# Moving the pw1 pair of chunk five, half B, behind the pw2 product of half A, in a two-layer Conformer and differential-attention trunk

## Reference

```python
def conformer_conv(h, pw1_w, pw1_b, dw_w, dw_b, ln_g, ln_b, pw2_w, pw2_b):
    u = h @ pw1_w + pw1_b                       # 1024 -> 2048
    a, gate = jnp.split(u, 2, axis=-1)
    u = a * jax.nn.sigmoid(gate)
    u = lax.conv_general_dilated(u, dw_w[:, None, :], ..., padding=((30, 0),),
                                 feature_group_count=1024) + dw_b      # causal, 31 taps, per channel
    u = jax.nn.silu(layernorm(u, ln_g, ln_b))
    return u @ pw2_w + pw2_b                    # 1024 -> 1024

x = x + conformer_conv(rmsnorm(x, conv_norm_g), ...)
x = x + (silu(h @ w1) * (h @ w3)) @ w2          # h = rmsnorm(x, ffn_norm_g); 2816 hidden channels
```

## Time and profile before

| | |
|---|---|
| median of 3 runs | 2310.55 us (2309.19, 2310.55, 2311.31) |
| profiled execution | span 2310.0 us (the page gives no other time of its own) |
| PE busy | 2252.5 us, 98% |
| DVE busy | 1673.4 us, 72% |
| ACT busy | 903.3 us, 39% |
| chain that ended last | PE 89%, DVE 8%, ACT 1%, issue 1% |
| HBM | 87 GB/s over the span |

### The profile page before, as it was taken

How to read it: one execution, slowest core, us unless ns; L and a number is a source line. 1 busy time by engine, 2 the same in 40 slices (tenths; PEclk the granted TensorE clock), 3 DMA queues, 4 the chain that set the end, 5 groups by cost and what they waited for, 6 DMA issues and landing times.

```text
span 2310.0 us, 27735 instructions
## 1 busy us (share of the span) xinstructions
PE 2252.5 (98%) x10517; PEld 1826.9 (79%) x10517; DVE 1673.4 (72%) x2617; ACT 903.3 (39%) x1597; POOL 68.6 (3%) x51
## 2 busy tenths in 40 slices
PE   7999989999999999999999999999999999999998
PEld 6885768888888888887777777878788888887886
DVE  6997689999666634345677777674778888877874
ACT  5221532222354422223455555564443332325443
POOL 0000000000000000002111111000000000000000
PEclk9999999999999999999999999999999999999999
DMA  4110223333333333333111111111023333329552
GB/s 141 47 37 19 73 72 93 96 93 95 94 98 91 101 95 95 103 89 84 37 37 37 37 37 37 62 60 44 28 81 101 100 107 105 104 98 325 195 163 88
DMA packets 287666, 202.13 MB, mean 88 GB/s; under 512 B 9045, under 2 KB 254126, under 8 KB 287534
## 3 DMA queue, kind: packets, MB, share of 16 engines
q1 hardware_dynamic: 287534, 200.36, 28.4%
HBM read 174.37 MB, written 25.95 MB: 87 GB/s over the span
## 4 chain that ended last, share of the span: by engine, by line
PE 89%; DVE 8%; ACT 1%; issue 1%; DMA 0%; SPq 0%; DVEq 0%; ACTq 0%
PE ps L2271 27%; PE ps L2273 26%; PE ps L2272 26%; PE ps L2409 3%; PE ps L2254 3%; DVE cacc L1620 2%; DVE cvA L1620 2%; PE ps L2367 1%; DVE sc L1871 1%; PE ps L2326 0%; DVE Wl L1545 0%; ACT sc L1297 0%; DVE Sl L1786 0%; PE ps L2336 0%; DVE rstd L1558 0%
## 5 line engine op out<-in xcount | busy, mean ns | idle before, releaser
L2271 PE MATMUL ps<-Sh,Wl 128*128 128x512 f32 x1616 | 655.8, 406 | 16.4 <-DVE Sl L1708 6.8
L2273 PE MATMUL ps<-Sh,Wh 128*128 128x512 f32 x1616 | 632.7, 392 | 0.0
L2272 PE MATMUL ps<-Sl,Wh 128*128 128x512 f32 x1616 | 631.9, 391 | 0.0
L2271 PEld LDWEIGHTS ps<-Sh,Wl 128*128 128x128 f32 x1616 | 305.1, 189 | 94.6 <-issue 33.3
L2273 PEld LDWEIGHTS ps<-Sh,Wh 128*128 128x128 f32 x1616 | 304.6, 188 | 65.8
L2272 PEld LDWEIGHTS ps<-Sl,Wh 128*128 128x128 f32 x1616 | 305.3, 189 | 59.7 <-issue 3.4
L1545 DVE TENSOR_TENSOR Wl<-raw,Wh 128x1024 fp32r<-128x1024 f32 (+1 forms) x178 | 213.3, 1198 | 87.2 <-ACT Wh L1084 86.3
L1084 ACT ACTIVATE Wh<-raw 128x1024 fp32r<-128x1024 f32 (+1 forms) x178 | 183.3, 1032 | 153.3 <-DMA raw<-in_ffn_w_dram 126.2
L2271 PE MATMUL ps<-G0h,Wl 128*128 128x512 f32 x352 | 138.6, 394 | 0.0
L2273 PE MATMUL ps<-G0h,Wh 128*128 128x512 f32 x352 | 137.0, 389 | 0.0
L2272 PE MATMUL ps<-G0l,Wh 128*128 128x512 f32 x352 | 137.0, 389 | 0.0
(11 more groups left out here) (273 smaller groups left out, 3869.6 us busy)
## 6 DMA issues: line engine op xcount, KB each, us to landing
raw<-in_ffn_w_dram SPq DMA_DIRECT2D x130, 512.0 KB, 3.8
raw<-in_pw_w_dram SPq DMA_DIRECT2D x32, 512.0 KB, 3.9
raw<-in_ffn_w_dram SPq DMA_DIRECT2D x32, 448.0 KB, 3.7
draw<-in_ffn_w_dram SPq DMA_DIRECT2D x55, 256.0 KB, 4.5
raw<-in_ffn_w_dram SPq DMA_DIRECT2D x36, 256.0 KB, 4.2
graw<-t_dram SPq DMA_DIRECT2D x36, 256.0 KB, 4.9
graw<-g_dram SPq DMA_DIRECT2D x33, 256.0 KB, 4.3
g_dram<-st SPq DMA_DIRECT2D x27, 256.0 KB, 2.0
```

Source lines behind the costliest of these rows:

```text
L2271: pe.matmul(dst, ll, rh, start=start, stop=False)
L2272: pe.matmul(dst, lh, rl, start=False, stop=False)
L2273: return pe.matmul(dst, lh, rh, start=False, stop=stop)
```

## The change

The pair of products (5,B) is taken out of the first stage. Its two weight blocks are loaded a second time as blocks AGAIN and AGAIN + 1 behind the eight pw2 blocks, and its two products run behind pw2 of half A and ahead of F0A, into banks 6 and 7. The sum over partitions for half A's norm stands inside the first of these products, after four of its eight chunks. The gate's sigmoid is the last thing ACT does ahead of F0A and goes to sq; the glu (`glu_behind`) is done by DVE in step 0 of F0A. `slot` and `slot_before` keep the ring: the two blocks take slots 2 and 3, behind the last two pw2 blocks, so that the first two F0A blocks keep slots 0 and 1. Splits are placed by hand: `lo(AGAIN)` after pw2_out of chunk 6, `lo(AGAIN + 1)` and `lo(F0A.block0)` ahead of the reciprocal, `lo(F0A.block0 + 1)` in the middle of the Sl loop; on ACT `hi(AGAIN + 1)` and `hi(F0A.block0)` stand ahead of the root, around the loading of its table.

```diff
@@ -96,7 +96,8 @@
 
 PW1 = 0
 PW2A = PW1 + 2 * KC
-F0A = Ffn(0, (LA,), (8, 7, 7), PW2A + KC, 5 * KC, 0, 0, 0, True)
+AGAIN = PW2A + KC
+F0A = Ffn(0, (LA,), (8, 7, 7), AGAIN + 2, 5 * KC, 0, 0, 0, True)
 PW2B = F0A.block0 + F0A.blocks()
 F0B = Ffn(0, (LB,), (8, 7, 7), PW2B + KC, F0A.result0 + F0A.results() + KC, FC, 0, 3 * KC, False)
 ATT0 = F0B.block0 + F0B.blocks()
@@ -196,9 +197,19 @@
     return UBANKS[q % len(UBANKS)]
 
 
+def slot(b):
+
+    return (b if b < AGAIN else b + 2) % RING
+
+
+def slot_before(b):
+
+    return b - {AGAIN: 2, AGAIN + 1: 2, AGAIN + 2: 6, AGAIN + 3: 6}.get(b, RING)
+
+
 def uslot(q):
 
-    return (q + 2 * (TAIL % RING)) % USLOTS
+    return (q + 2 * slot(TAIL)) % USLOTS
 
 
 def down_slot(d):
@@ -222,17 +233,29 @@
 DIAGS = 22
 
 
+BEHIND = LATE - 1
+
+
 def pair(n, hf):
 
-    return 2 * n + hf if n < LATE else 2 * LATE + 2 * hf + n - LATE
+    return PAIRS1.index((n, hf))
+
+
+PAIRS1 = [(n, hf) for n in range(BEHIND) for hf in (LA, LB)] + [(n, LA) for n in range(BEHIND, KC)] + \
+    [(n, LB) for n in range(LATE, KC)] + [(BEHIND, LB)]
+
+
+def pair_before(n, hf):
+
+    return pair(n - 2 if (n, hf) == (LATE, LB) else n - 1, hf)
 
 
 def results_through(b):
 
     if b < PW2A:
-        return 2 * pair(b // 2, LB) + b % 2 + 1
+        return 2 * pair(b // 2, LA if b // 2 == BEHIND else LB) + b % 2 + 1
     if b < F0A.block0:
-        return 4 * KC + b - PW2A + 1
+        return 4 * KC - 2 + b - PW2A + 1
     if b < PW2B:
         return F0A.result0 + b - F0A.block0 + 1
     if b < F0B.block0:
@@ -703,10 +726,10 @@
             return HEADS - 1 if WO0 <= b < WO0 + KC else KC
 
         def ring_hi(b):
-            return Wh[b % RING][:, 0:down_size(b), :]
+            return Wh[slot(b)][:, 0:down_size(b), :]
 
         def ring_lo(b):
-            return Wl[b % RING][:, 0:down_size(b), :]
+            return Wl[slot(b)][:, 0:down_size(b), :]
 
         def step_done(engine, d):
 
@@ -938,6 +961,8 @@
 
             for n in range(KC):
                 load(PW2A + n, cols(pw2, n))
+            load(AGAIN, cols(pw1, KC + BEHIND))
+            load(AGAIN + 1, cols(pw1, BEHIND))
             ffn(F0A)
             for n in range(KC):
                 load(PW2B + n, cols(pw2, n))
@@ -1070,14 +1095,14 @@
 
                 if b >= BLOCKS:
                     return
-                s = b % RING
+                s = slot(b)
                 n = down_size(b)
                 if ATT0 <= b < WO0:
                     act.wait_ge(raw_ok, b - ATT0 + 1)
                 else:
                     act.wait_ge(raw_in[b % 2], 16 * (b // 2 + 1))
                 if b >= F1.block0 + RING or RING <= b < F1.block0:
-                    act.wait_ge(mm, results_through(b - RING))
+                    act.wait_ge(mm, results_through(slot_before(b)))
                 elif b >= F1.block0:
 
                     act.wait_ge(wo_mm, result_at(KC - 4 + s, LB) + 1 if s else 4 * KC)
@@ -1120,7 +1145,7 @@
             def gate(n, hf):
                 act.wait_ge(mm, 2 * pair(n, hf) + 1)
                 if n:
-                    act.wait_ge(u_ok, pair(n - 1, hf) + 1)
+                    act.wait_ge(u_ok, pair_before(n, hf) + 1)
                 act.activation(tmp[:, hf, :], ps[:, 2 * hf, :], ACT.Sigmoid,
                                bias=col("pw1_b", KC + n)).then_inc(sig_ok, 1)
 
@@ -1134,6 +1159,8 @@
                     if n == 1 and hf == LA:
                         act.wait_ge(lam_s, 2)
                         act.activation(lexp, lsum, ACT.Exp).then_inc(lam_e, 1)
+                    if (n, hf) == (BEHIND, LB):
+                        continue
                     gate(n, hf)
                     if n in (1, 2):
                         x_copies(8 * (n - 1) + 4 * hf)
@@ -1181,13 +1208,21 @@
             gate(CONV_PE, LB)
 
             for n in range(KC):
-                hi(PW2A + n + 2)
+                if n < KC - 1:
+                    hi(PW2A + n + 2)
                 squares(SUM_F0A, n, X(n, LA), x_ok, n + 1)
+            hi(AGAIN + 1)
             act.activation(spare, eps, ACT.Sqrt)
+            hi(F0A.block0)
             root(1, LA, SUM_F0A)
             for n in range(KC):
                 act.wait_ge(fx_ok, n + 1)
                 act.activation(Sh[:, LA, n, :], tmp[:, n % 4, :], ACT.Copy, scale=col("ffn_norm_g", n)).then_inc(s_hi, 1)
+                if n == 3:
+                    hi(F0A.block0 + 1)
+            act.wait_ge(mm, F0A.result0 - 1)
+            act.wait_ge(acc_ok, squares_added(SUM_F0A, KC - 1))
+            act.activation(sq[:, 0, :], ps[:, 6, :], ACT.Sigmoid, bias=col("pw1_b", KC + BEHIND)).then_inc(sig_ok, 1)
 
             def ffn(f, beside):
                 for i, (g, what, c, b) in enumerate(f.order()):
@@ -1635,7 +1670,7 @@
                         dve.tensor_tensor(neg_lam, lexp[:, 1:2], lexp[:, 0:1], ALU.subtract).then_inc(lam_s, 1)
                         dve.wait_ge(lam_s, 4)
                         dve.tensor_scalar(neg_lam, neg_lam, -LAMBDA_INIT, None, ALU.add).then_inc(lam_s, 1)
-                    if i == 8 and n < LATE:
+                    if i == 8 and n < BEHIND:
                         glu(n, LB)
                     if n + 2 < KC:
                         lo0, lo1, glu0 = (16, 24, 28) if n + 1 < LATE else (9, 16, 14)
@@ -1683,17 +1718,22 @@
             glu(CONV_PE, LB)
 
             def pw2_out(hf, n):
-                r = (F0A.result0 if hf == LA else F0B.result0) - KC + n
+                r = (F0A.result0 - 2 if hf == LA else F0B.result0) - KC + n
                 dve.wait_ge(mm, r + 1)
                 dve.scalar_tensor_tensor(X(n, hf), by_block(ps[:, n % 4, :]), col("pw2_b", n), X(n, hf),
                                          ALU.add, ALU.add).then_inc(x_ok, 1)
 
             for n in range(KC):
-                lo(PW2A + n + 2)
+                if n < KC - 2:
+                    lo(PW2A + n + 2)
                 pw2_out(LA, n)
                 if n >= 2:
                     add_square(SUM_F0A, n - 1)
+                if n == KC - 2:
+                    lo(AGAIN)
             add_square(SUM_F0A, KC - 1)
+            lo(AGAIN + 1)
+            lo(F0A.block0)
             recip(1, LA)
             dve.wait_ge(rstd_ok, 2)
             for n in range(KC + 2):
@@ -1707,6 +1747,15 @@
                     dve.wait_ge(s_hi, OP_F0A * KC + m + 1)
                     dve.scalar_tensor_tensor(Sl[:, LA, m, :], tmp[:, m % 4, :], col("ffn_norm_g", m),
                                              Sh[:, LA, m, :].bitcast(F32), ALU.mult, ALU.subtract).then_inc(s_lo, 1)
+                if n == 5:
+                    lo(F0A.block0 + 1)
+
+            def glu_behind():
+
+                dve.wait_ge(mm, F0A.result0)
+                dve.wait_ge(sig_ok, pair(BEHIND, LB) + 1)
+                dve.scalar_tensor_tensor(upB[:, BEHIND, PAD:UP], ps[:, 7, :], col("pw1_b", BEHIND), sq[:, 0, :],
+                                         ALU.add, ALU.mult).then_inc(u_ok, 1)
 
             def ffn(f, beside):
                 def low(g, c, j, hf):
@@ -1758,6 +1807,8 @@
                             dve.tensor_tensor(X(c, hf), by_block(ps[:, bank, :]), X(c, hf), ALU.add).then_inc(add_ok, 1)
 
             def beside_f0a(i):
+                if i == 0:
+                    glu_behind()
                 for s in range(STEPS * i, min(STEPS * (i + 1), KC * CONV_OPS)):
                     conv(LB, s)
                 if i == CENTRE_AT:
@@ -2299,7 +2350,7 @@
                     if n == 0:
                         free, value = s_lo, KC * hf + 1 + what
                     else:
-                        free, value = (u_ok if what else sig_ok), pair(n - 1, hf) + 1
+                        free, value = (u_ok if what else sig_ok), pair_before(n, hf) + 1
                     dense(gate_block(n) + what, 2 * hf + what, Sh[:, hf], Sl[:, hf], KC, free, value, ready)
                     ready = None
                     yield what
@@ -2349,7 +2400,8 @@
             pw1_pair(0, LB)
             for n in range(1, LATE):
                 for hf in (LA, LB):
-                    pw1_pair(n, hf)
+                    if (n, hf) != (BEHIND, LB):
+                        pw1_pair(n, hf)
                     if n < 3:
                         x_raw(8 * (n - 1) + 4 * hf)
                 if n >= 3:
@@ -2375,7 +2427,13 @@
             for n in range(KC):
                 free, value = (u_ok, pair(CONV_PE, n // 2) + 1) if n < 4 else (x_ok, n - 3)
                 dense(PW2A + n, n % 4, Sh[:, LA], Sl[:, LA], KC, free, value, s_ready(OP_LN_A * KC) if n == 0 else None)
-            sum_up(SUM_F0A)
+
+            def sum_beside(k):
+                if k == 4:
+                    sum_up(SUM_F0A)
+
+            for what in range(2):
+                dense(AGAIN + what, 6 + what, Sh[:, LB], Sl[:, LB], KC, cpe_ok, 1, None if what else sum_beside)
 
             def freed(f, r, first):
 
```

## The result

| | before | after |
|---|---|---|
| median | 2311.41 us (20 runs, 2308.93 to 2313.53) | 2315.15 us (20 runs, 2313.97 to 2316.47) |
| span of the profiled execution | 2310.0 us | 2313.3 us |

The ratio is 1.0017, with a 95% interval of 1.0011 to 1.0023: slower by 3.9 us, 2.5 to 5.3 (the two medians themselves differ by 3.7). The forecast was +4.1 us, 0.18%. The measured times lie inside the range that was given, and the change is within the 0.2% that was called the likeliest case. The total was right; the profile shows that two of its terms were not: the clock of the taps, and the clock of F0A's first product.

A forecast was written before the change was run, and what follows sets the result against it. DVE was taken to pace the first stage, though PE is busy 98% of the span. Glu -0.66, F0A's first product +3.2 and the first w2 stall +1.6 gave +4.1 on 2310.55: 2314.7 us, range 2311.8 to 2317.5.

The forecast's parts named there:

- the clock of the taps: Taps behind the mean of chunk 5: half speed at first, before and after the change alike; 0 us.
- the clock of F0A's first product: Product ahead of F0A's second: granted clock stays 1.00; losing its earlier half-clock stretch saves nothing, since it waited for Sl.
- The first stage gives back next to nothing: First stage: DVE paces it, so the pair's 10.88 us become PE idle time; only one glu's 0.66 us is saved.
- Splits ahead of the reciprocal: Behind pw2, ahead of F0A: lo(F0A.block0) waits for its hi and delays DVE's reciprocal; +2.05 us.
- The split in the Sl loop: DVE's Sl loop: lo(F0A.block0 + 1) behind the fourth Sl adds 1.13 us.
- F0A's first product, +3.2 in all: PE's first F0A product ends later with the last Sl, by 2.05 + 1.13: +3.2 us.
- The stall: First w2 product: PE waits for DVE's last G0l, 5.55 - 3.2 - 0.75 = 1.6 us.
- Rival 2: First w2 product: DVE's lateness is absorbed and PE doesn't stall; +2.5 us, 2313.1 us; chance 0.15.
- Rival 3: F0A's first product: the clock falls while PE's work is thinned by Sl waits; +5.9 us, 2316.5 us; chance 0.12.
- DVE's lateness of 5.55: Step 0 of F0A: table load and sigmoid delay the split, glu_behind adds 0.66; DVE's step 1 is 5.55 us late.
- -0.66: First stage: one glu leaves DVE's chunk 5; -0.66 us.
- Rival 4: First stage's end: new holes keep half clock through pair (7,A), ending after DVE; +8.7 us, 2319.2 us; chance 0.08.

The follow-up runs named there:

- the pair in both places: The changed kernel with pair (5,B) also computed at its old place in the first stage, result unused: 2314.41 us, ratio 1.0015.
- the pair taken out: The kernel before without pair (5,B) and with nothing put behind pw2; half B's chunk-5 convolution reads chunk 4's input: 2310.3 us, ratio 0.9998.
- late sigmoid: The changed kernel with the sigmoid moved to step 17 of F0A and glu_behind to step 20: 2314.12 us, ratio 1.0012.
- plain ring: The changed kernel with plain ring order behind pw2 and three splits done earlier, between pw2 results: 2314.28 us, ratio 1.0013.
- both repairs: The changed kernel with plain ring order, its three earlier splits, and sigmoid and glu moved to steps 17 and 20 of F0A: 2312.28 us, ratio 1.0006.
- the run whose clock stayed up: The changed kernel with pair (5,B) computed a second time at its old place: 2314.41 us, ratio 1.0015.
- the reordering: The changed kernel with the mean of chunk 5 behind the taps and DVE's splits and glus of half A's chunks 5 to 7 earlier: 2307.51 us, ratio 0.9982.
- all that was mended: The changed kernel with the reordering, both repairs, and the last split moved out of the Sl loop: 2302.71 us, ratio 0.9958.

## Why the prediction came out

**The first stage gives back next to nothing: shown.** The mean of chunk 5 came at 191.37 with 5.6 us of idle time before it (forecast 191.4 and some 6), and the pair could be computed there a second time for nothing. The other idle time, 4.1 us, stood inside pair (6,A), at its value product, and not between (6,A) and (7,A) as forecast.

**The clock of the taps as before, a term of 0: mis-sized.** From M to the mean behind the taps the kernel before took 30.37 us and the pair in both places 30.65, with 3.33 and 2.65 us of idle time ahead. The five kernels with 5.6 us ahead (the changed one, the pair taken out, late sigmoid, plain ring, both repairs) took 29.02 to 29.36. The term was -1.0 to -1.35 by these profiles. What differs is how long PE worked at half clock from M on: 5.7 us in the kernel before and 6.2 with the pair in both places, 2.9 to 3.6 in the five others. They come to it in two ways. In three of them (late sigmoid, plain ring, both repairs) the clock was at half for 6.8 us as in the kernel before, but 3.2 to 3.5 us of it had passed in the idle time. In the changed kernel and with the pair taken out it fell only 0.5 us ahead of M and was back after 3.4 us; in the kernel before it had fallen 1.2 us ahead. So "the clock falls earlier in a longer idle time" doesn't describe the changed kernel, and why its slow stretch was short stays open. Nor is it shown that the term belongs to the change: the two profiles of one kernel differ by 1.6 us over the same taps (28.50 and 26.88). Another 0.6 us up to W came of the changed kernel's clock in pair (7,B); that it belongs to the change isn't shown, since the same distance varies by 1 us between these profiles.

**Splits ahead of the reciprocal, +2.05: right.** Measured +1.9 (6.0 against 4.1), and moving them away gave back 1.7 of it at G.

**The split in the Sl loop, 1.13, and F0A's first product, +3.2 in all: right where the clock held, short where it fell.** +3.06 in the run whose clock stayed up, +3.99 in the changed kernel.

**The stall, 1.6: right by itself, 0.74 in the profile.** With the clock up it was 1.68. The last hidden split came 5.70 us late against W where 5.55 was forecast. Rival 2, no stall, is out.

**Rival 3.** Its condition was met, the clock fell in the thinned product, and I had given that 0.12. Its price was wrong. I had worked it out as a product late by 6.6 us that takes the stall in: 3.2, and 3.4 for the clock. The clock cost 0.93, since it was at half for only 3.4 us and PE's waits for Sl in that time went into it. The product was late by 4.0, and the 0.93 was taken out of PE's wait for DVE: W to the last chunk of the first w2 product is 111.69 and 111.68 us with and without it. The sum behind W, forecast 4.8, is 4.9 at that place and 5.05 at G either way. The total held because the stall term was what DVE is late beyond PE: 3.2 + 1.6 is DVE's lateness of 5.55 less the slack of 0.75, and stays 4.8 as long as PE is late by less than that.

**The sum.** Forecast -0.66 + 4.8 = +4.1. By the marks -0.66 - 1.2 (taps' clock) + 5.05 = +3.2, and in this profile -2.69 + 5.05 = +2.4 at G and 3.3 over the whole span. Measured +3.9 with 2.5 to 5.3. So what stands behind W was forecast for the right reason, and part of how near the total came is luck: a term taken as 0 for the clock of the taps was -1.0 to -1.35 in the profiles, and nothing here says what makes up the difference between the marks and the medians; it is inside the interval. Rival 4 didn't occur: one stretch at half clock fell into pair (6,A), where it was hidden.

## What to carry to other kernels

Work that is moved into an idle gap is free for the engine that idles, but its weight splits, its nonlinearity and its product with the gate land on the engines whose lateness made the gap; price those first. Where the work came from matters as much: if another engine paces that stage, freed time is worth nothing until that engine's queue is reordered too (here the change is +3.9 us without the reordering and -4.2 with it, and -9.7 with all that was mended; taking the pair out and doing it nowhere gave only -0.5). And follow each chain of lateness to the place where the two engines meet, rather than adding them: there the later one counts, and what the other loses to the clock on the way is free as long as it still arrives first (0.93 us in the changed kernel; once DVE's lateness was mended, it was paid).

## What was not expected of the hardware

Behind a hole of 1.44 us between short bursts of work (0.68 us in every 1.27), TensorE's granted clock fell from 1.00 to 0.50 for 3.4 us in seven of eight profiles that had it; in the eighth the same hole passed at 1.00. In the one profile without it PE was busy for 0.70 us of a slice of 1 us, and the clock stayed up. What decides it isn't shown.

Two executions of one kernel can take the same wait differently: after 2.28 us the clock was at half in one and at full in the other. The execution that was slower at the taps was the faster one at W, by 2.7 us; 1.7 of it are there behind the next wait, which was shorter and passed at full clock.
